# Where the queries of the next head are made in a product-key expert stage

## The reference

```python
q = (hc @ w_pq).reshape(PEER_CHUNK, PEER_HEADS, 2, PEER_DK_HALF)
sc = jnp.einsum('thcd,chnd->thcn', q, sub_keys).astype(jnp.float32)
vals, idx = lax.top_k(sc, PEER_TOPK)
cand = vals[:, :, 0, :, None] + vals[:, :, 1, None, :]
cand_idx = idx[:, :, 0, :, None] * N_KEYS + idx[:, :, 1, None, :]
top_s, top_c = lax.top_k(cand.reshape(...), PEER_TOPK)
experts = jnp.take_along_axis(cand_idx.reshape(...), top_c, axis=-1)
g = jax.nn.softmax(top_s, axis=-1)
ue = peer_u[experts]
ve = peer_v[experts]
act = jax.nn.gelu(jnp.einsum('td,thkd->thk', hc, ue).astype(jnp.float32), approximate=False)
return jnp.einsum('thk,thkd->td', (g * act).astype(ve.dtype), ve)
```

## Time and profile before

| | us |
|---|---|
| median of 3 runs | 2957.98 (2957.88 to 2959.83) |
| profiled execution, its own time | 2962.33 |
| its span | 2960.6 |
| first product of the peer stage's head 0 | 898.79 |
| of head 1 | 1023.09 |
| of head 7 | 1524.44 |
| first instruction of the group stage | 1607.2 |
| TensorE, VectorE, ScalarE, GpSimd busy, share of the span | 82%, 59%, 31%, 33% |

### The profile page before, as it was taken

One profiled execution on the slowest core, in us unless ns is written; L12 is line 12 of the kernel. 1 busy time (PEld: TensorE's weight loads), 2 busy tenths in 40 slices (PEclk: granted clock), 3 DMA queues, 4 the chain that ended last, 5 costly groups with the idle time before them and its releaser, 6 DMA issues. The chain is left out here.

```text
span 2960.6 us, 30510 instructions
## 1 busy us (share of the span) xinstructions
PE 2435.0 (82%) x9839; PEld 1621.2 (55%) x9839; DVE 1750.1 (59%) x3659; ACT 908.2 (31%) x1740; POOL 982.8 (33%) x691
## 2 busy tenths in 40 slices
PE   6997999878887888989887996898667477569897
PEld 4776878767663344433333664565345345336675
DVE  3444311032135998888885588678669878865151
ACT  4443222233221322222222333154134324323232
POOL 2331545343232334443443233324323532310000
PEclk9998999989998999999889997899778678769898
DMA  4321333123038899999999899899889999964643
GB/s 157 100 67 48 95 100 106 62 102 111 27 114 344 319 390 416 416 415 390 401 406 416 343 381 360 309 368 395 326 343 389 412 410 394 377 263 172 222 171 141
DMA packets 255194, 797.77 MB, mean 269 GB/s; under 512 B 18141, under 2 KB 139637, under 8 KB 189525
## 3 DMA queue, kind: packets, MB, share of 16 engines
q0 software_dynamic: 73728, 536.90, 45.0%
q1 hardware_dynamic: 181333, 259.25, 25.1%
HBM read 787.26 MB, written 14.07 MB: 271 GB/s over the span
## 5 line engine op out<-in xcount | busy, mean ns | idle before, releaser
L1337 POOL DMA_INDIRECT gathered<-in_peer_rows,experts x436 | 531.6, 1219 | 900.5 <-DVE x_res L2654 592.9
L1695 PE MATMUL peer_banks<-gathered,peer_diags 128*128 128x512 f32 x720 | 339.9, 627 | 51.0 <-ACT peer_diags L1750 50.9
L78 PE MATMUL group_banks<-group_x_t,group_ring 128*128 128x128 f32 (+1 forms) x2016 | 343.8, 334 | 20.8 <-ACT group_x_t L2466 8.4
L78 PEld LDWEIGHTS group_banks<-group_x_t,group_ring 128*128 128x128 f32 x2016 | 309.8, 210 | 52.3 <-ACT group_x_t L2466 10.8
L2640 DVE CUSTOM_DVE_ANT_0 gathered<-gathered,late_nat 128x1024 f32<-128x1024 f32 x256 | 317.8, 1244 | 30.5 <-DMA gathered<-in_peer_rows,experts 28.1
L2654 DVE SCALAR_TENSOR_TENSOR x_res<-gathered,group_weights,x_res 128x1024 f32<-128x1024 f32 x256 | 329.7, 1288 | 2.5
L1695 PEld LDWEIGHTS peer_banks<-gathered,peer_diags 128*128 128x128 f32 x720 | 143.0, 202 | 237.3 <-issue 237.2
L2276 PE MATMUL group_banks<-group_ring,group_x_t 128*128 128x512 f32 x512 | 234.4, 612 | 12.9 <-DMA group_ring<-in_weights 12.8
L1790 DVE CUSTOM_DVE_ANT_0 peer_product<-gathered,early_nat 128x1024 f32<-128x1024 f32 x180 | 214.6, 1221 | 40.1 <-DMA gathered<-in_peer_rows,experts 39.9
L1695 PE MATMUL peer_banks<-early_gathered,peer_diags 128*128 128x512 f32 x304 | 150.5, 648 | 47.8 <-ACT peer_diags L1750 47.8
L1743 ACT ACTIVATE peer_acts<-peer_dots 128x2 f32<-128x2 f32 x128 | 26.0, 203 | 489.9 <-DVE peer_dots L1790 489.7
(11 more groups left out here) (379 smaller groups left out, 4229.6 us busy)
## 6 DMA issues: line engine op xcount, KB each, us to landing
group_ring<-in_weights SPq DMA_DIRECT2D x270, 512.0 KB, 7.8
mixer_wq<-in_w_in SPq DMA_DIRECT2D x24, 512.0 KB, 4.2
mixer_wk<-in_w_in SPq DMA_DIRECT2D x24, 512.0 KB, 4.7
peer_w<-in_w_pq SPq DMA_DIRECT2D x8, 1024.0 KB, 15.2
gathered<-in_peer_rows,experts POOLq DMA_INDIRECT x436, 11.0
diff_wv<-in_w_in SPq DMA_DIRECT2D x8, 512.0 KB, 4.2
conv_wb<-in_w_in SPq DMA_DIRECT2D x8, 512.0 KB, 4.1
merge_w<-in_w_conv_out SPq DMA_DIRECT2D x8, 512.0 KB, 4.5
```

Of the source, the lines that this page charges most:

```text
L78: last = nc.tensor.matmul(out, lhsT, rhs, start=n == 0, stop=n == len(pairs) - 1)
L1337: nc.gpsimd.indirect_dma_start(row_buffer(m, r), None, A["peer_rows"], bass.IndirectOffsetOnAxis(ap=at, axis=0))\
L1695: last = nc.tensor.matmul(ps[:, ACC[unit % 2] + half, :], diags[:, r % DIAGS, :], row_buffer(m, r)[:, D + half * BANK:D + (half + 1) * BAN ...
```

## The change

The order of the heads in which choices are made is now 1, 2, ..., 7, 0, and position i of that order is made entirely during head i of the rows. The queries are cut into eight pieces of two matmuls, one before each of the rows 2 to 9; the keys are turned at row 9, the scores made at row 11. ScalarE copies the operands at lot 5 and the scores at lot 6. VectorE chooses at lots 7, 9, 11 and 13, exponentials come at lots 10 and 14 and the softmaxes one lot later. In position 7 head 0 is made for tiles 2 and 3 alone, with 256 columns, and its choices stand at lots 9 and 11. SyncE and GpSimd issue the same DMAs in the same order of use, with counts adapted; the semaphore counts of experts and gates become functions (`chosen`, `gates_before`).

```diff
@@ -1609,18 +1609,29 @@
     ROWS_HERE = UNITS * TOPK
     DIAGS = 8
     PH = Routing.PH
-    CHOSEN = 1
     Q, KEYS, SCORES, ACC = (0, 1), 2, (2, 3), (4, 6)
-    SCORES_AT = [(0, 2, 4, 6), (1, 10, 12, 14), (2, 20, 24, 28)], [(2, 2, 8, 18)]
-    COPIES_AT = [(0, 3, 4), (1, 7, 8), (2, 13, 15)], [(2, 7, 11)]
-    CHOOSE_AT = {5: (0, 2), 7: (0, 3), 9: (1, 0), 11: (1, 1), 13: (1, 2), 15: (1, 3)}, {3: (1, 0), 6: (1, 1), 9: (1, 2), 12: (1, 3)}
-    GATES_AT = {8: (0, 1), 12: (1, 0), 16: (1, 1)}, {7: (1, 0), 13: (1, 1)}
+    ORDER = list(range(1, HEADS)) + [0]
+    LATE = slice(2 * P, 4 * P)
+    QUERY_AT, SCORES_AT = range(2, 10), 11
+    OPERANDS_AT, COPIES_AT = 5, 6
+    CHOOSE_AT = [{7: 0, 9: 1, 11: 2, 13: 3}] * (HEADS - 1) + [{9: 2, 11: 3}]
+    GATES_AT = [{10: 0, 14: 1}] * (HEADS - 1) + [{12: 1}]
+
+    def chosen(h, t):
+
+        if h:
+            return T * (h - 1) + t + 2
+        return 1 if t == 1 else T * (HEADS - 1) + t
+
+    def gates_before(h, n):
+
+        return 2 * h - 1 + n if h else (2 * HEADS - 1) * n
 
     def gates_at(lot):
 
 
-        return [(ahead + h, n) for h in range(HEADS) for at, (ahead, n) in GATES_AT[min(h, 1)].items()
-                if h * NT * LOTS + at == lot and ahead + h < HEADS]
+        i, at = divmod(lot, NT * LOTS)
+        return [(ORDER[i], GATES_AT[i][at])] if lot >= 0 and at in GATES_AT[i] else []
 
     with ctx:
         ps = banks()
@@ -1642,12 +1653,12 @@
         with nc.Block(no_gpsimd_drain=True) as block:
             @block.sync
             def _(sp):
-                for h in range(HEADS):
-                    if h:
-                        sp.wait_ge(q_done, h)
+                for i, h in enumerate(ORDER):
+                    if i:
+                        sp.wait_ge(q_done, i)
                     sp.dma_start(w[:, :, :], b.w_view[:, :, h * PH:(h + 1) * PH]).then_inc(w_loaded, 16)
-                    if h:
-                        sp.wait_ge(keys_turned, h)
+                    if i:
+                        sp.wait_ge(keys_turned, i)
                     sp.dma_start(keys[:, :, :], b.key_view[h * N_KEYS:(h + 1) * N_KEYS, :, :]).then_inc(keys_loaded, 16)
...
             def _(pe):
-                def query(h, c):
-                    if c == 0:
-                        pe.wait_ge(w_loaded, 16 * (h + 1))
-                        if h:
-                            pe.wait_ge(q_copied, h)
-                    made = accumulate(nc, ps[:, Q[c], :], [(w[:, k, c * P:(c + 1) * P], h_t[:, k, :]) for k in range(KC)])
-                    if c == 1:
+                def tokens(i):
+                    return slice(0, S) if i + 1 < HEADS else LATE
+
+                def query(i, n):
+
+                    c, quarter = divmod(n, 4)
+                    if n == 0:
+                        pe.wait_ge(w_loaded, 16 * (i + 1))
+                        if i:
+                            pe.wait_ge(q_copied, i)
+                    for k in range(2 * quarter, 2 * quarter + 2):
+                        made = nc.tensor.matmul(ps[:, Q[c], tokens(i)], w[:, k, c * P:(c + 1) * P], h_t[:, k, tokens(i)], start=k == 0, stop=k == KC - 1)
+                    if n == 7:
                         made.then_inc(q_done, 1)
 
-                def turn_keys(h):
-                    pe.wait_ge(keys_loaded, 16 * (h + 1))
-                    if h:
-                        pe.wait_ge(scores_ready, 2 * h)
+                def turn_keys(i):
+                    pe.wait_ge(keys_loaded, 16 * (i + 1))
+                    if i:
+                        pe.wait_ge(scores_ready, 2 * i)
                     b.turn_keys(nc, ps[:, KEYS, :], m.ident).then_inc(keys_turned, 1)
 
-                def score(h):
-                    pe.wait_ge(q_copied, h + 1)
-                    pe.wait_ge(keys_ready, h + 1)
-                    for n in range(2):
+                def score(i):
+                    pe.wait_ge(q_copied, i + 1)
+                    pe.wait_ge(keys_ready, i + 1)
+                    for n in range(2) if i + 1 < HEADS else [1]:
                         b.score(nc, ps[:, SCORES[n], :], (2 * n, 2 * n + 1))
 
...
-                    h, at = divmod(r, NT * TOPK)
-                    for ahead, first_half, second_half, scores in SCORES_AT[min(h, 1)]:
-                        if h + ahead < HEADS:
-                            if at == first_half:
-                                query(h + ahead, 0)
-                            if at == second_half:
-                                query(h + ahead, 1)
-                                turn_keys(h + ahead)
-                            if at == scores:
-                                score(h + ahead)
+                    i, at = divmod(r, NT * TOPK)
+                    if at in QUERY_AT:
+                        query(i, QUERY_AT.index(at))
+                        if at == QUERY_AT[-1]:
+                            turn_keys(i)
+                    if at == SCORES_AT:
+                        score(i)
                     add_row(r)
...
-                def copy_operands(h):
-                    act.wait_ge(q_done, h + 1)
-                    if h:
-                        act.wait_ge(scored, 2 * h)
+                def copy_operands(i):
+                    tokens = slice(0, S) if i + 1 < HEADS else LATE
+                    act.wait_ge(q_done, i + 1)
+                    if i:
+                        act.wait_ge(scored, 2 * i)
                     for c in range(2):
-                        last = nc.scalar.activation(q_t[:, c, :], ps[:, Q[c], :], ACT.Copy)
+                        last = nc.scalar.activation(q_t[:, c, tokens], ps[:, Q[c], tokens], ACT.Copy)
                     last.then_inc(q_copied, 1)
-                    act.wait_ge(keys_turned, h + 1)
+                    act.wait_ge(keys_turned, i + 1)
                     nc.scalar.activation(keys_t[:, :, :], ps[:, KEYS, 0:2 * P].rearrange("p (c n) -> p c n", c=2), ACT.Copy)\
                         .then_inc(keys_ready, 1)
 
-                def copy_scores(h):
-                    for n in range(2):
-                        act.wait_ge(scored, 2 * h + n + 1)
-                        if h >= 2:
-                            act.wait_ge(expert_done, T * (h - 1) - CHOSEN)
-                        b.copy_scores(nc, ps[:, SCORES[n], :], h, n)
+                def copy_scores(i):
+                    for count, n in enumerate(range(2) if i + 1 < HEADS else [1]):
+                        act.wait_ge(scored, 2 * i + count + 1)
+                        if i >= 2:
+                            act.wait_ge(expert_done, chosen(ORDER[i - 2], T - 1))
+                        b.copy_scores(nc, ps[:, SCORES[n], :], i, n)
 
                 def exps(h, n):
 
-                    act.wait_ge(shifted_ready, T * h + 2 * n + 2 - CHOSEN)
-                    if h:
-                        act.wait_ge(gates_ready, 2 * h + n - 1)
+                    act.wait_ge(shifted_ready, chosen(h, 2 * n + 1))
+                    if gates_before(h, n):
+                        act.wait_ge(gates_ready, gates_before(h, n))
                     nc.scalar.activation(powers[:, 2 * n:2 * n + 2, :], m.shifted[:, 2 * n:2 * n + 2, :], ACT.Exp).then_inc(exp_done, 1)
 
...
-                    for ahead, operands, scores in COPIES_AT[min(h, 1)]:
-                        if h + ahead < HEADS:
-                            if at == operands:
-                                copy_operands(h + ahead)
-                            if at == scores:
-                                copy_scores(h + ahead)
-                    for ahead, n in gates_at(lot):
-                        exps(ahead, n)
+                    if at == OPERANDS_AT:
+                        copy_operands(i)
+                    if at == COPIES_AT:
+                        copy_scores(i)
+                    for h, n in gates_at(lot):
+                        exps(h, n)
...
+                def choose(i, t):
+                    h, n = ORDER[i], t // 2
+                    if h == 0:
+                        used = exp_done, gates_before(HEADS - 1, 1) + 1
+                    elif h == 1:
+                        used = (exp_done, 1) if n == 0 else None
+                    else:
+                        used = exp_done, gates_before(h - 1, n) + 1
+                    dve.wait_ge(scores_ready, 2 * i + n + 1 if h else 2 * i + 1)
+                    b.choose(nc, dve, m, h, t, used, kept=b.scores[:, i % 2, t, :, :])
+
                 b.choose(nc, dve, m, 0, 1, kept=m.first_scores)
                 softmax(0, 0)
                 for lot in range(UNITS * LOTS):
-                    h, at = divmod(lot, NT * LOTS)
+                    i, at = divmod(lot, NT * LOTS)
                     n = lot % LOTS
                     inner_products(lot)
                     if lot:
                         weigh(lot - 1)
                     if n == 4 and lot >= LOTS:
                         add_unit(lot // LOTS - 1)
-                    if at in CHOOSE_AT[min(h, 1)]:
```

(9 more changed lines are left out.)

15 lines of the change are left out of this document (8 added, 7 removed).

## The result

The changed kernel took 3063.24 us (median of 4 runs, 3054.17 to 3066.96), against 2957.93 us of the kernel before on the same chip: ratio 1.0351, 95% interval 1.0333 to 1.037. The profiled execution's own time is 3062.81 us, its span 3061.0, which is 100.4 us more than before. Of the executions behind the medians further down, one of the ten of e1_pieces took 10633 us and is left out of its ratio.

The account below looks back on a forecast made before the run. Gathers of expert rows bound the kernel; the change makes a loop. Head 0 -15.7, six heads +120.3, last head +4.7, rest -1 sum to +108.3 us, from 2957.98 to 3066; 8 in 10 range 3030 to 3095.

Parts of the forecast that it names:

- TensorE's lag at row 0: Middle heads: TensorE starts row 0 at T + 10.7 us, T being the start of VectorE's product for row 0.
- slow restart: TensorE after its pause, before row 0: half-clock records make the restart 13.2 us instead of 10.3, 2.9 a head.
- Queries, scores, choice: Middle heads: queries ready at T + 39.9 us, first scores copied at T + 45.6, VectorE standing still about 25.
- hidden loop: Rival: scores ready when VectorE reaches lot 7, middle heads stay DMA-bound at 83.6 us; kernel about 2942; chance 0.07.
- From the first choice on: Middle heads: VectorE alone sets the pace, 58.0 us from first choice to next head, gathers not holding it.
- Head 0: First head: first scores copied at 949.4, wait for weights stays, head 1 starts at 1007.4 instead of 1023.09, -15.7 us.
- Head 7: Last head, with tiles 2 and 3 of head 0 made under it: 87.5 us instead of 82.8, +4.7.
- The rest: Weight loads and GpSimd's waits at nothing; group stage gains 1 us because row gathers have already landed.
- GpSimd's wait for experts: GpSimd: its waits fall on choices made well before; without that cover, at most 7.8 us.
- Shorter loop: Rival: TensorE reaches row 0 with 0 to 5 us lag, heads 93 to 98 us, kernel 3002 to 3032; chance 0.06.
- Slower clock: Rival: idle TensorE stays at half clock into rows and queries, kernel 3096 us and more; chance 0.03.
- No difference: Rival: pieces neither help nor hurt, head 0's gain meets a loop of 86 us, kernel 2958; chance 0.02.

Follow-up runs that it names:

- e1_pieces: Kernel before, with queries from head 1 on cut into the change's eight pieces, still two heads ahead; 2955.98 us, ratio 0.9997.
- e5_half: Changed kernel with only the first of each piece's two query matmuls from position 1 on; 3018.89 us, ratio 1.0212.
- e3_first: Changed kernel with, from position 1 on, queries before row 0, scores at row 2, copies at lots 1 and 2, choices at 6, 8, 10, 12; 3032.14 us.
- e3b_first: As e3_first, but ScalarE copies operands and scores at lots 5 and 6 again; 3035.93 us, ratio 1.0267.
- e3c_first: As e3b_first, but both ScalarE copies stand at lot 4; 3002.26 us, ratio 1.0138.
- e6: Changed kernel with scores made one position ahead and choices spread over the head again, same head order and pieces; 2944.28 us, ratio 0.9953.
- e4_split: Changed kernel with choices for tiles 2 and 3 moved to lots 1 and 3 of the next head, their exponential at lot 5; 3024.21 us.

## Why the prediction was right

The forecast was 3066 us, the measurement 3063.24; the mechanism is in the traces, and most of its terms are. That the two lie 3 us apart is in part luck. In the profiles the terms forecast as +108.3 us sum to +100.4; 5 of those 8 us don't show in the medians, which differ by 105.3, because the profiled execution of before stood 4.35 us above its median and that of the change 0.4 below.

**TensorE's lag at row 0.** Predicted T + 10.7. The restart is at 1209.56, T - 2.3 (predicted T - 2.5); the 32 records up to 1224.91 hold eight rows, the last two of which (3.43 us) are rows 0 and 1, so row 0 begins at 1221.5, T + 9.6. The slow restart cost 24 records 11.9 us where 10.3 would do: 1.6 us (1.5 to 2.0 in the six heads), where I took 2.9. This is the largest error in the loop, and 6 x 1.1 = 6.6 us is the difference between +120.3 and +113.7. The Trainium skill, "TensorE: Matmul & The Clock Gate", Part 1, "What's actually happening", advises against fitting a count of cold matmuls, the penalty being under 1% of a span. For what lies on the path the trace agrees in size: 1.6 x 6 = 9.6 us is 0.3% of 3061. It is nonetheless a real term of each period, and a little over half of what I gave it.

**Queries, scores, choice.** Queries ready at T + 38.8 (predicted 39.9), first choice at T + 44.4 (45.6): after the lag, nothing on the path is off by more than 0.1 us. e5_half shows the query records on the path one to one. Off the path a reading failed: I had VectorE at the end of lot 7 by T + 21 and idle for about 25 us, some 20 of them in front of a weighing. In head 3 the products from row 8 on waited 7.9 us for gathers, VectorE was there at T + 28.8, and it then waited 11.73 us for the weighing and 3.75 for the scores. It was covered here. But the rival *hidden loop* would have needed the scores by about T + 29 in this order and not by T + 25.

**From the first choice on.** 57.9 us against 58.0, with no product waiting for a gather. e5_half repeats it, and e3_first, e3b_first and e3c_first give 60.3 to 60.5 with one lot more behind it (2.4 to 2.6 us more, a lot being 2.37).

**Head 0**: head 1 started 16.7 us earlier than before (1006.40 less 1023.09), against -15.7; 1.6 of that is the earlier start of the stage, which was not forecast. VectorE's first choice came at 948.18 against 949.4. The forecast took the wait for the weights as fixed; it was 6.71 us in this execution, which fits, and 0.67 to 4.10 in others with the same head 0. **Head 7** +3.9 against +4.7. **The rest:** the gain of 1 us at the group stage did not come. The wait for final_g (6.08 us) is still there:

```profile
1712.64 3.74 PE L2241 MATMUL group_banks<-group_affine,group_ones 1*128 1x512 f32 x4 [6.16 <-DMA group_affine<-in_final_g]
```

but the reason that I gave for a gain was wrong before that: the row gathers are not over when the stage begins. GpSimd issues them up to 1701.13, and the DMA share is 1.01 and 1.02 in the two stretches from 1700 to 1709, as before the stage in the kernel before (1.03 and 1.01 from 1600 to 1608). Whether the wait hangs on gathers queued ahead is therefore not shown. GpSimd's wait for experts, put at 7.8 us at most, was 12.1 us once, at 1684.85, for a gather of the group stage; the stage from 1708.18 on was 0.6 us shorter all the same.

**The rivals.** *Hidden loop*, from 2942: at first sight e6 measures that number, but it does so because it takes the loop out; with the loop in, no run came below 2989. Its stated threshold, scores by T + 25, was never reached by a kernel with the loop. The Trainium skill, "Perfetto Trace Analysis", "Optimization Strategy", says interleaving regimes may improve performance; here e1_pieces shows that the finer interleaving of queries and rows is worth nothing measurable, in heads whose DMA share was 1.0 before, and the change, which interleaves them with a short dependence, cost 3.5%. *Shorter loop*: the lag was 9.6, not 0 to 5. *Slower clock*: the granted clock fell to 0.85 to 0.87 in the middle heads (0.92 before), but by the pauses after the scores (0.75 from 1254.54 to 1314); between 1224.91 and 1254.54 it was 1.00, and every piece took 1.88 us. The low mean stands where TensorE has slack, and its only price is the 1.6 us above. *No difference* needed a loop of 86 us; the best one without a score in reserve had 91.8.

What I did not see before the experiments: ScalarE's ring of diagonals and its exponential. They cost nothing in the change: no wait of ScalarE for a buffer of the ring stands in its list, and VectorE, for which the exponentials at lots 10 and 14 are made, works from the first choice to the next head without a wait. They made three of my expectations wrong by 40 to 48 us each, always in the same way: I had followed TensorE and VectorE and taken ScalarE to be free because it is busy 20 us of 102.

## What to carry to other kernels

Before moving a producer closer to its consumer, write down the cycle it closes over one iteration, across all in-order engines, and add it up: here 44.4 us from a head's start to the first choice and 57.9 from there to the next start, 102.3 against the 83.6 us of a head that the gathers bound. If the sum is over the present bound, keep one result in reserve; the other parts of the edit may then still pay, as in e6_ahead. And follow the least busy engine's instruction order as closely as the busiest one's: a copy that others wait for must not stand behind anything that waits for them.

## What the runs showed of the hardware

- A switch of ScalarE's function costs its table load, 1.28 us, and no more here: in the rows of e4_split, the exponential begins at 1225.59, 1.29 after the load's start, and the gelu at 1227.13, 1.29 after the second's. The Trainium skill, "ScalarE: Activation LUTs", "What ACT_TABLE_LOAD costs", gives the same 1.28 us for the load and adds a drain of 1.38; that drain is not to be seen here, and the measured rows decide.
- Cutting an accumulation of eight 512-column f32 matmuls into four pieces of two, with matmuls into other banks between them, costs TensorE nothing: pieces and rows follow one another after 1.72 us, which is 4 x 0.43.
- TensorE pays for a pause after the pause: eight records took 6.48 us at 1268.45 behind 6.81 us of idling (granted clock 0.50 from 1268.4 to 1271.5, the 1.2 GHz level), and the next eight, from 1274.77 on, 3.60 at 1.00 (2.4 GHz). One row alone took 3.51 us behind a pause of 2.96 in e4_split (granted clock 0.53), instead of 1.88.
